# Stage o of a ten-layer network: transposes and products of the attention one step further behind the scores

## What is computed

```python
def odd_mixer(t, w_in, ...):
    proj = t @ w_in
    y_c = s5_ssm(proj[..., :o1], ...)
    y_d = mla_attention(proj[..., o1:o2], proj[..., o2:o3], proj[..., o3:], ...)
    return jnp.concatenate([y_c, y_d], axis=-1) @ w_out

def mla_attention(...):
    # 6 heads, q and k of 128 + 64 (rotary), v of 128; scale = 192 ** -0.5
    def block(i, qb):                      # 4 blocks of 128 queries
        sc = jnp.einsum('bqhd,bkhd->bhqk', qb, k) * scale
        p = jax.nn.softmax(jnp.where(chunk_causal_mask(i, s), sc, -jnp.inf), axis=-1)
        return jnp.einsum('bhqk,bkhd->bqhd', p, v)
```

## Time and profile before

| | |
|---|---|
| profiled execution | 2985.41 us |
| its span in the trace | 2983.6 us |
| TensorE matmuls busy | 2888.5 us (97%) |
| TensorE weight loads busy | 2376.8 us (80%) |
| VectorE busy | 1736.0 us (58%) |
| ScalarE busy | 1108.0 us (37%) |
| GpSimd busy | 246.1 us (8%) |
| chain of work that ended last | TensorE 87%, VectorE 6%, ScalarE 4% |

### The profile page before, as it was taken

The page is one execution under the profiler, slowest core; times in us unless marked ns, Lnnn a source line. Parts: engine busy times, 40 slices in busy tenths (PEclk is TensorE's granted clock), DMA queues, the critical chain, the costliest instruction groups (busy, mean ns, idle before and its releaser), DMA issues.

```text
span 2983.6 us, 38082 instructions
## 1 busy us (share of the span) xinstructions
PE 2888.5 (97%) x13878; PEld 2376.8 (80%) x13878; DVE 1736.0 (58%) x2631; ACT 1108.0 (37%) x1680; POOL 246.1 (8%) x280
## 2 busy tenths in 40 slices
PE   8999999999999999999999999889999988999998
PEld 6888887888788888878888876588888875888887
DVE  5554535875688676644555586565444576464435
ACT  4332324553465432233322324343222445332222
POOL 1000000000100100000000100024510100110001
PEclk9999999999999999999999999999999999999999
DMA  4322232222212333332322321013332310223332
GB/s 148 99 92 92 89 102 78 64 64 82 81 57 64 93 92 99 99 92 92 99 92 92 100 85 43 22 57 122 97 98 86 98 57 22 64 87 97 98 93 91
DMA packets 70398, 252.10 MB, mean 84 GB/s; under 512 B 7808, under 2 KB 9856, under 8 KB 69632
## 3 DMA queue, kind: packets, MB, share of 16 engines
q1 hardware_dynamic: 68112, 241.89, 26.1%
q10 hardware_dynamic: 2016, 7.96, 0.8%
q0 software_dynamic: 144, 0.52, 0.0%
HBM read 248.25 MB, written 2.10 MB: 84 GB/s over the span
## 4 chain that ended last, share of the span: by engine, by line
PE 87%; DVE 6%; ACT 4%; issue 2%; POOL 1%; ACTq 0%; DVEq 0%; POOLq 0%
PE ps L297 18%; PE ps L298 18%; PE ps L299 18%; PE ps L568 2%; PE ps L569 2%; PE ps L570 2%; PE ps L790 2%; PE ps L876 2%; ACT w_high L277 1%; PE ps L792 1%; PE ps L791 1%; DVE w_low L284 1%; PE ps L1841 1%; PE ps L591 1%; PE ps L1422 1%
## 5 line engine op out<-in xcount | busy, mean ns | idle before, releaser
L284 DVE TENSOR_TENSOR w_low<-raw,w_high 128x1024 fp32r<-128x1024 f32 x456 | 567.4, 1249 | 445.2 <-ACT w_high L277 438.9
L297 PE MATMUL ps<-h_high,w_high 128*128 128x512 f32 x1872 | 736.9, 394 | 3.4 <-DVE arena L1006 1.7
L299 PE MATMUL ps<-h_high,w_low 128*128 128x512 f32 x1872 | 729.6, 390 | 0.0
L298 PE MATMUL ps<-h_low,w_high 128*128 128x512 f32 x1872 | 729.4, 390 | 0.0
L277 ACT ACTIVATE w_high<-raw 128x1024 fp32r<-128x1024 f32 x456 | 477.8, 1051 | 450.6 <-PE ps L299 204.6
L297 PEld LDWEIGHTS ps<-h_high,w_high 128*128 128x128 f32 x1872 | 352.3, 188 | 75.4 <-DVE arena L1006 2.5
L299 PEld LDWEIGHTS ps<-h_high,w_low 128*128 128x128 f32 x1872 | 351.8, 188 | 73.9
L298 PEld LDWEIGHTS ps<-h_low,w_high 128*128 128x128 f32 x1872 | 352.1, 188 | 70.0
L297 PE MATMUL ps<-y_high,w_high 128*128 128x512 f32 x640 | 251.0, 392 | 0.6 <-DVE y_low L1976 0.2
L298 PE MATMUL ps<-y_low,w_high 128*128 128x512 f32 x640 | 249.5, 390 | 0.0
L299 PE MATMUL ps<-y_high,w_low 128*128 128x512 f32 x640 | 249.3, 390 | 0.0
(11 more groups left out here) (455 smaller groups left out, 4595.0 us busy)
## 6 DMA issues: line engine op xcount, KB each, us to landing
raw<-stream SPq DMA_DIRECT2D x456, 512.0 KB, 3.6
table<-tables_in ACTq DMA_DIRECT2D x5, 1088.0 KB, 6.4
x<-x_in ACTq DMA_DIRECT2D x8, 256.0 KB, 8.1
x_out<-x SPq DMA_DIRECT2D x16, 128.0 KB, 1.7
const<-const_in SPq DMA_DIRECT2D x1, 673.0 KB, 7.9
arena<-ssm_in POOLq DMA_DIRECT2D x1, 512.0 KB, 5.7
params<-params_in ACTq DMA_DIRECT2D x1, 287.0 KB, 6.6
```

The source lines that it names most:

```text
L284: nc.vector.tensor_tensor(w_low[:, u.slot], raw[:, u.raw], w_high[:, u.slot].bitcast(F32), ALU.subtract).then_inc(weights_low, 1)
L297: nc.tensor.matmul(bank, wh, high[:, k], start=k == 0, stop=False)
L298: nc.tensor.matmul(bank, wh, low[:, k], start=False, stop=False)
L299: mm = nc.tensor.matmul(bank, wl, high[:, k], start=False, stop=k == tiles - 1)
```

## The change

The transposes run three steps behind the scores and the products four (before: two and three), and there is one step more. The weights, maxima, sums and inverses have three places: the two tiles of `o_p` and a third, which is an unused stretch of constants for the first eight blocks and `root` after them. The turned weights have a second tile, `rstd`, used by even blocks from the fifth on. Waits follow; TensorE has a new one ahead of the transposes, ScalarE one for the recurrence's state at block 4.

```diff
-        O_STEPS = NBLK * MLA_HEADS + 3
+        O_STEPS = NBLK * MLA_HEADS + 4
...
-        o_wt = work[:, 0:T]
+        o_spare = con("chunk", 3 * P, 3 * P)
...
-        o_neg, o_sum, o_inv = ([o_col[:, 2 * n + q:2 * n + q + 1] for q in range(2)] for n in range(1, 4))
+        o_soft_col = table[:, 4 * T + 32:4 * T + 41]
+        o_neg, o_sum, o_inv = ([o_soft_col[:, 3 * n + q:3 * n + q + 1] for q in range(3)] for n in range(3))
...
-            s, w, t, v = (m if 0 <= m < O_BLOCKS else None for m in (n, n - 1, n - 2, n - 3))
+            s, w, t, v = (m if 0 <= m < O_BLOCKS else None for m in (n, n - 1, n - 3, n - 4))
...
+        def o_weights(n):
+
+            if n % 3 < 2:
+                return o_p[:, n % 3]
+            return o_spare if n < 2 * NBLK else root[:]
+
+        def o_turned_weights(n):
+
+            return rstd[:] if n % 2 == 0 and n >= NBLK else work[:, 0:T]
...
                     if tr is not None:
                         pe.wait_ge(o_scaled, tr + 1)
+                        if tr > 0:
+                            pe.wait_ge(o_wt_copied, tr)
                         for kb in range(tr % NBLK + 1):
                             mm = nc.tensor.transpose(ps[:, 6, kb * P:(kb + 1) * P],
-                                                     o_p[:, tr % 2, kb * P:(kb + 1) * P], ident)
+                                                     o_weights(tr)[:, kb * P:(kb + 1) * P], ident)
...
                         act.wait_ge(o_t_done, tr + 1)
-                        if tr > 0:
-                            act.wait_ge(o_pv, tr)
-                        nc.scalar.activation(o_wt[:, 0:width], ps[:, 6, 0:width], ACT.Copy).then_inc(o_wt_copied, 1)
+                        if tr == NBLK:
+                            act.wait_ge(o_ssm, O_SSM * O_SUPER)
+                        elif tr > 0:
+                            act.wait_ge(o_pv, tr if tr < NBLK else tr - 1)
+                        nc.scalar.activation(o_turned_weights(tr)[:, 0:width], ps[:, 6, 0:width], ACT.Copy).then_inc(o_wt_copied, 1)
...
             def inverse(n):
                 dve.wait_ge(o_exp, n + 1)
-                if n >= 2:
-                    dve.wait_ge(o_scaled, n - 1)
-                nc.vector.reciprocal(o_inv[n % 2], o_sum[n % 2]).then_inc(o_inverse, 1)
+                if n >= 3:
+                    dve.wait_ge(o_scaled, n - 2)
+                nc.vector.reciprocal(o_inv[n % 3], o_sum[n % 3]).then_inc(o_inverse, 1)
...
-                        if s >= 2:
-                            dve.wait_ge(o_exp, s - 1)
-                        nc.vector.tensor_scalar(o_neg[s % 2], o_max, -192 ** -0.5, None, op0=ALU.mult).then_inc(o_soft, 1)
+                        if s >= 3:
+                            dve.wait_ge(o_exp, s - 2)
+                        nc.vector.tensor_scalar(o_neg[s % 3], o_max, -192 ** -0.5, None, op0=ALU.mult).then_inc(o_soft, 1)
```

More of the change, by code:

```diff
@@ L2351, in o_tensor @@
                             mm = nc.tensor.matmul(ps[:, o_pv_bank(h), b * P:(b + 1) * P], o_v[:, kb, h * P:(h + 1) * P],
-                                                  o_wt[:, kb * P:(kb + 1) * P], start=kb == 0, stop=kb == b)
+                                                  o_turned_weights(v)[:, kb * P:(kb + 1) * P], start=kb == 0, stop=kb == b)
                         mm.then_inc(o_pv, 1)
@@ L2461, in o_scalar @@
                         width = (w % NBLK + 1) * P
-                        p = o_p[:, w % 2, 0:width]
+                        p = o_weights(w)[:, 0:width]
                         act.wait_ge(o_inverse, w + 1)
-                        nc.scalar.activation(p, p, ACT.Copy, scale=o_inv[w % 2]).then_inc(o_scaled, 1)
+                        nc.scalar.activation(p, p, ACT.Copy, scale=o_inv[w % 3]).then_inc(o_scaled, 1)
                     if s is not None:
@@ L2467, in o_scalar @@
                         act.wait_ge(o_soft, O_SOFT * (s + 1))
-                        nc.scalar.activation(o_p[:, s % 2, 0:width], ps[:, o_score_bank(s), 0:width], ACT.Exp,
-                                             bias=o_neg[s % 2], scale=192 ** -0.5, accum_out=o_sum[s % 2]).then_inc(o_exp, 1)
+                        nc.scalar.activation(o_weights(s)[:, 0:width], ps[:, o_score_bank(s), 0:width], ACT.Exp,
+                                             bias=o_neg[s % 3], scale=192 ** -0.5, accum_out=o_sum[s % 3]).then_inc(o_exp, 1)
                 if event == "square":
```

## The result

The changed kernel takes 2993.61 us (median of 20 runs, 2985.97 to 2999.9), the kernel before 2982.84 us in the same series (20 runs, 2979.05 to 2988.08). The ratio is 1.0033, 95% interval 1.0024 to 1.0041: slower by 10 us, a third of a percent. On a second chip the same pair gives 1.0026 (1.0016 to 1.0035). The forecast was +1.0 us on a median of 2986.18 us; on the median of these 20 runs it would be 2983.8 us. 2993.61 lies outside its range either way.

What follows compares the result with a forecast made beforehand. TensorE, busy 81.83 of 96.00 us in the steps, was held by one wait per head for ScalarE's copy. Terms 0 - 0.9 - 0.5 + 0.7 + 0.2 + 1.5 gave +1.0 us: 2987.2 us, range 2982.8 to 2990.5.

Steps and rivals of the forecast that it cites:

- The start: Steps 2 to 7: path to the small products shorter by 0.5 us, then +0.55 in step 7; together 0.
- the marks up to step 11: Steps 8 to 12, VectorE the bound: its low half moves behind the maximum of step 11, which starts 0.9 us sooner.
- steps 16 to 19: Saving of 0.9 us lost waiting at the gate projection for VectorE's low half, more work in steps 18 and 19: +0.7 us.
- The drain: Extra step bare at the end: 5.83 us from VectorE's last start to the last product, against 4.33 before: +1.5 us.
- the tiles and waits: Third places, second turned tile and 23 more TensorE waits: taken as 0, at most 2.5 us for issue.
- The central point: Transposes no longer wait for the scaling; products wait for ScalarE's copy as long or longer, up from 8.2 us.
- steps 20 to 23: No transpose waits; less work under the covered wait, with a copy 0.10 us shorter: +0.23 us.
- steps 13 to 15: Transposes' waits and lower clock lie here: between nothing and 1.0 us more saved, taken as -0.5 us.
- once more: Rival: the clock falls once more, at the step with 128 columns: +2.6 us, 2988.8 us; chance 0.20.
- with four: Rival: four more clock falls, three in heads and one longer in the drain: +7.4 us, 2993.6 us; far slower, chance 0.03.
- One of the prediction's own signs of being wrong: The forecast would be wrong if the stretch of the attention steps ended 3 us sooner or later.
- The rival of a lower clock: Longer TensorE gaps at the 128-column step make the clock fall: one more fall 2988.8 us, chance 0.20; four 2993.6, 0.03.

Runs made afterwards that it cites:

- two copies: Kernel before with two unread ScalarE copies (512 and 128 columns) ahead of the copy of the turned weights in steps 8, 12, 16 and 20: 2985.11 us, ratio 1.0012.

## Why the prediction was wrong

**The sum of the parts** was right in the main. The start came out at -0.74 where -0.5 stood, the marks up to step 11 at -0.99 where -0.9 stood, steps 16 to 19 at +0.66 where +0.7 stood, with the gate projection behind VectorE's low half. The drain at full clock took 5.84 us where 5.83 stood, and the tiles and waits cost nothing that can be measured. The central point holds too: the products are waited for longer and the transposes no more. One term was too small at full clock already: steps 20 to 23 stood at +0.23, of which the wait was to be 0.10 us shorter, but the time from the maximum of block 19 to the product of step 21 grew by 0.48 us, because VectorE's low half moved ahead of the gate. The prediction had seen that move for steps 8 to 12 and not here. The order costs 1 to 2 us by two estimates; +1.0 was forecast.

**The step that failed** is the clock. I priced it in one term, "between nothing and 1.0 us more, I take -0.5" for steps 13 to 15, counted no fall anywhere else in the sum, and gave its rival "once more" 0.20 and its rival "with four" 0.03. The trace shows 18 us more at 1.2 GHz and the runs of the second chip 16, which is 5 to 6 us of time; steps 13 to 15 alone came out at +3.1 us where -0.5 stood. One of the prediction's own signs of being wrong came true with it: the stretch of the steps ended more than 3 us later. The unread matmuls, which raise the clock and save no work, give back 8.4 us.

The rival of a lower clock was right in kind and got far too small a chance. That its version with four falls named 2993.6 us is luck in part. It stood for +7.4 us on 2986.18, and the measured rise is 10 us on 2982.84; and it counted four more falls, where the trace has one more and three that last longer. Two errors kept its chance small. I took the price of a fall from those before (about 3 us at the low level, 1.6 us of time); in the changed kernel one lasts ten microseconds. And I saw that gaps of 0.91 and 1.81 us had brought falls in two heads, worked out gaps of up to 1.8 and 1.5 us for steps 13 and 17, and still put the clock at a gain of 0.5 us. The gaps found are 1.69 us in step 13 and 2.62 in step 21, with long falls behind them, and 1.49 in step 17, with none.

The rule that I had quoted is that small idle times between groups of matmuls, if frequent, make the clock swing (the Trainium skill, page TensorE: Matmul & The Clock Gate, section "A second HAM failure mode: psum-queue depth-cycling"). The trace agrees: the mean clock of the steps is 0.83 against 0.91.

**What stays open** is which feature of the new order lowers the clock. Unread work in the heads gives back 3 to 5 us, in the drain alone nothing that can be measured, in both 8; lengthened gaps in the old order have no effect on the clock that is clear of noise.

## What to carry to other kernels

Where a stretch of TensorE's work is made of short groups with waits between them, count the idle time of each gap and what stands in front of it, for its own length and for the clock: here, moving work out of a covered wait cost 1 to 2 us for itself and 5 to 6 us by the clock. When one engine's work moves a step later, look at every chain that it now stands ahead of, as the low half did with the gate. Making a pipeline deeper adds a bare step at its end and does not shorten a wait whose two ends keep their distance; look for the pair (here exponential and copy, and the one PSUM bank of the transposes) that decides. A matmul that nobody reads, into a free bank and no longer than the gap, is a cheap test of whether the clock is at work, and on the kernel before it was a gain of 3 to 4 us.

## What the runs showed of the hardware

The low level can outlast the gap by far while TensorE is busy. In the changed kernel, behind the gap of 1.69 us at 2508.36 the clock was 0.55 and then 0.50 over ten microseconds in which the records show TensorE busy for 5.00 of 5.00 us twice (products, transposes and scores of 128 to 384 columns, each with its own weights); in the kernel before a fall at the same step came to three and a half (0.95 and 0.70). The same came back with lengthened gaps in the old order (0.51, 0.50, 0.62).

The length of a gap alone did not decide whether a fall followed. Falls came with gaps of 0.91 and 1.81 us in the kernel before, of 1.59, 1.69 and 2.62 in the heads of the changed one, and of 1.62 with two copies. In the two microseconds behind gaps of 1.00 and 1.38 us in the kernel before, 1.49 in the changed one, and 1.98 and 2.53 with two copies the clock stayed at 1.00.

And the same program lands on either side from run to run: the changed kernel's 20 runs spread over 13.9 us, with mean clocks of 0.977 to 0.983, while the kernel before spreads over 9.0 us.
